# The rwkv scan of a two-block model: the two directions set eight steps apart, the backward preparation put behind the forward one, and the rates of the keys kept

## What is computed

```python
def _wkv7_step(S, inp):
    r, w, k, v, kk, a = inp
    sa = jnp.einsum('bhvk,bhk->bhv', S, kk)
    S = S * w[:, :, None, :] - sa[..., None] * (kk * a)[:, :, None, :] + v[..., None] * k[:, :, None, :]
    y = jnp.einsum('bhvk,bhk->bhv', S, r)
    return S, y
...
    decay = jnp.exp(-jnp.exp(w_log))
    a = jax.nn.sigmoid((a0[:, None, None, :] + la).astype(jnp.float32))
...
    kd = kf[None] * (1.0 + (a - 1.0) * k_a)
...
    _, y_fwd = lax.scan(_wkv7_step, S0, (r_t, tm(decay[0]), tm(kd[0]), v_t, kk_t, tm(a[0])))
    _, y_bwd = lax.scan(_wkv7_step, S0, (r_t, tm(decay[1]), tm(kd[1]), v_t, kk_t, tm(a[1])), reverse=True)
...
    kdh = (kd[0] + kd[1]).reshape(B, L, H, N)
    bonus = jnp.sum(rh * kdh * r_k, -1, keepdims=True) * v.reshape(B, L, H, N).astype(jnp.float32)
    out = ((y + bonus.reshape(B, L, D)) * g).astype(x.dtype)
```

## Time and profile before

| | |
|---|---|
| median of three runs | 2638.3 us (2636.0 to 2647.1) |
| the profiled execution | 2632.1 us, its span 2630.3 us |
| TensorE busy | 2522.9 us (96%), 23502 matmul records |
| VectorE, ScalarE, GpSimd busy | 1991.4, 1538.5, 52.5 us |
| mean granted clock of TensorE | 0.973 |
| chain that ended last | TensorE 88%, VectorE 6%, ScalarE 3%, DMA 1%, issue 1% |
| HBM | 533.8 MB read, 203 GB/s over the span |

### The profile page before, as it was taken

How to read it: one execution, slowest core, us unless ns; L and a number is a source line. 1 busy time by engine, 2 the same in 40 slices (tenths; PEclk the granted TensorE clock), 3 DMA queues, 4 the chain that set the end, 5 groups by cost and what they waited for, 6 DMA issues and landing times.

```text
span 2630.3 us, 54618 instructions
## 1 busy us (share of the span) xinstructions
PE 2522.9 (96%) x23502; PEld 2344.5 (89%) x23502; DVE 1991.4 (76%) x3044; ACT 1538.5 (58%) x2505; POOL 52.5 (2%) x58
## 2 busy tenths in 40 slices
PE   8999999988989999999999999999998899999999
PEld 8779998867887899999999999999897799998999
DVE  4545547765544699999999999999877788575884
ACT  4435435444423577777777777777665565464663
POOL 0001100000000000000000000000003000000000
PEclk9889999978998999999999999999999999999999
DMA  6123452300002499999999999999832255451443
GB/s 245 71 73 120 167 188 103 112 1 3 20 4 90 164 362 343 359 347 363 340 368 335 372 336 368 338 373 336 312 132 102 81 193 180 174 186 55 169 179 127
DMA packets 83258, 538.48 MB, mean 205 GB/s; under 512 B 9488, under 2 KB 9616, under 8 KB 38976
## 3 DMA queue, kind: packets, MB, share of 16 engines
q1 hardware_dynamic: 82368, 530.68, 54.7%
q0 software_dynamic: 640, 4.22, 0.4%
HBM read 533.81 MB, written 1.05 MB: 203 GB/s over the span
## 4 chain that ended last, share of the span: by engine, by line
PE 88%; DVE 6%; ACT 3%; issue 1%; DMA 1%; DVEq 0%; SPq 0%; PEldq 0%; ACTq 0%
PE ps L575 24%; PE ps L576 23%; PE ps L577 23%; PE ps L1465 2%; PE ps L581 1%; PE ps L590 1%; DVE sl L533 1%; PE ps L1995 1%; PE ps L1400 1%; PE ps L1450 1%; PE ps L1459 1%; PE ps L818 1%; PE ps L1421 1%; PE ps L2140 1%; PE ps L1443 1%
## 5 line engine op out<-in xcount | busy, mean ns | idle before, releaser
L2222 DVE TENSOR_TENSOR sl<-ring,sh 128x1024 fp32r<-128x1024 f32 x613 | 718.2, 1220 | 13.7 <-ACT sh L2180 10.9
L2180 ACT ACTIVATE sh<-ring 128x1024 fp32r<-128x1024 f32 x613 | 608.9, 1061 | 1.3 <-DVE xl L2065 1.3
L575 PE MATMUL ps<-sh,xh 128*128 128x256 f32 (+2 forms) x2012 | 568.9, 283 | 2.1 <-DVE sl L533 1.2
L577 PE MATMUL ps<-sh,xl 128*128 128x256 f32 (+2 forms) x2012 | 568.3, 282 | 0.0
L576 PE MATMUL ps<-sl,xh 128*128 128x256 f32 (+2 forms) x2012 | 567.9, 282 | 0.0
L575 PE MATMUL ps<-xh,sh 128*128 128x256 f32 (+2 forms) x1856 | 537.0, 289 | 24.5 <-DVE sl L533 12.8
L576 PE MATMUL ps<-xl,sh 128*128 128x256 f32 (+2 forms) x1856 | 532.0, 287 | 0.0
L577 PE MATMUL ps<-xh,sl 128*128 128x256 f32 (+2 forms) x1856 | 528.8, 285 | 0.0
L533 DVE TENSOR_TENSOR sl<-ring,sh 128x1024 fp32r<-128x1024 f32 (+1 forms) x341 | 401.0, 1201 | 80.9 <-ACT sh L526 80.5
L526 ACT ACTIVATE sh<-ring 128x1024 fp32r<-128x1024 f32 (+1 forms) x341 | 338.9, 1021 | 112.1 <-PE ps L577 105.4
L575 PEld LDWEIGHTS ps<-sh,xh 128*128 128x128 f32 x2012 | 378.3, 188 | 11.8 <-DVE sl L533 1.5
(11 more groups left out here) (552 smaller groups left out, 3887.2 us busy)
## 6 DMA issues: line engine op xcount, KB each, us to landing
ring<-ws_d SPq DMA_DIRECT2D x229, 1024.0 KB, 7.1
ring<-ws_d SPq DMA_DIRECT2D x80, 1536.0 KB, 6.4
ring<-ws_d SPq DMA_DIRECT2D x225, 512.0 KB, 6.5
ring<-ws_d SPq DMA_DIRECT2D x24, 1408.0 KB, 6.0
ring<-ws_d SPq DMA_DIRECT2D x4, 1256.0 KB, 5.6
ring<-ws_d SPq DMA_DIRECT2D x2, 1088.0 KB, 4.8
scan_t<-scn_d POOLq DMA_DIRECT2D x1, 1844.0 KB, 7.7
ring<-ws_d SPq DMA_DIRECT2D x1, 1248.0 KB, 5.2
```

What stands on the lines that cost most here:

```text
L575: e.matmul(out, ah, bh, start=start, stop=False)
L577: return e.matmul(out, al, bh, start=False, stop=stop)
L2180: e.activation(out, raw(u)[:, a:z], ACT.Copy).then_inc(*af.on("high", u, i))
L2222: e.tensor_tensor(l, raw(u)[:, a:z], f32(h), SUB).then_inc(s_fd if i < 2 else s_fp, 1)
```

## The change

The scan gets another order and the bonus another source for the rates.

- `streams`: six steps of forward alone, one of backward, four times backward and forward, one of backward; then the round with the bonus. At its beginning forward has done 10 steps and backward 6. Forward ends its short chunk in the first eight rounds, so that from then on it is eight steps behind backward, and the last eight rounds are forward's alone (75 rounds instead of 67).
- The rates are kept: forward's Sigmoid writes them to `Yb` (after the mix that still reads `DP` there), and backward's preparation adds its own (L1671 after the change). The bonus takes the sum from `Yb`, over 256 tokens instead of 272. Its two matmuls, two Sigmoids and the addition for each tile are gone, and it takes three rounds for a tile instead of four.
- The late mixes come in two lots of four instead of 3, 3 and 2.
- Unused matmuls: 12 behind forward's and 10 ahead of each direction's first G, where 20 stood ahead of forward's.

```diff
@@ -1151,7 +1151,7 @@
         def late_dve(w, e):
-            for ks in ((0, 1, 2), (3, 4, 5), (6, 7), (), (), ()):
+            for ks in ((0, 1, 2, 3), (4, 5, 6, 7), (), (), (), ()):
                 for k in ks:
@@ -1353,8 +1353,8 @@
-        PREPARE, LEAD = 6, 7
-        VV, va1, gate = KK, HW, Rr
+        PREPARE, LEAD = 6, 6
+        VV, gate = KK, Rr
         oc, nw = columns(out_weights())
@@ -1369,9 +1369,11 @@
                 next(runs[0])
-            for _ in range(PREPARE):
-                for g in (runs[0], runs[1], runs[0]):
-                    next(g)
+            next(runs[1])
+            for _ in range(PREPARE - 2):
+                next(runs[1])
+                next(runs[0])
+            next(runs[1])
             runs.append(bonus())
@@ -1401,9 +1403,10 @@
                 yield
+                if n == 0:
+                    warm_pe(w, e, "decays", 12)
                 yield
-                if n == 0:
-                    warm_pe(w, e, "prepared", 20)
+                warm_pe(w, e, ("prepared", n), 10)
                 w.wait_ge(dv["prepared", n, 1], IN_CON)
@@ -1514,18 +1517,10 @@
                 for k in range(8):
-                    for n in range(2):
-                        b, free = psum.take(("out a", n, k))
-                        w.wait_ge(*free)
-                        e.matmul(PS[:, b, 0:T0], sn("a2")[64 * n:64 * n + 64, 128 * k:128 * k + 128], HA[64 * n:64 * n + 64, :], start=True, stop=True).then_inc(
-                            *pe.on("out a", n, k))
                     yield
-                    if k:
-                        colsum_pe(w, e, ("quad", k - 1), "blk", VV[:, k - 1:k, :], 1, T0, dv["quad", k - 1])
-                    for _ in range(3):
-                        yield
-                yield
-                colsum_pe(w, e, ("quad", 7), "blk", VV[:, 7:8, :], 1, T0, dv["quad", 7])
+                    yield
+                    yield
+                    colsum_pe(w, e, ("quad", k), "blk", VV[:, k:k + 1, C0:T0], 1, T1, dv["quad", k])
                 for _ in range(BEFORE_GATES):
@@ -1547,10 +1542,12 @@
                     d0 = slice(4 * hf, 4 * hf + 4)
-                    t1, t2 = d.t1[hf], d.t2[hf]
+                    t1, t2 = d.t1[hf], d.t2[hf] if n else Yb[:, 4 * hf:4 * hf + 4, :]
                     for name, dst, bias in (("w2", t1, f"w0{n}"), ("a2", t2, f"a0{n}")):
...
                             w.wait_ge(pe[name, n, hf, i])
+                            if n == 0 and name == "a2":
+                                w.wait_ge(dv["mixed", 5, 4 * hf + i])
                             e.activation(dst[:, i, :], PS[:, psum[name, n, hf, i], 0:T0], ACT.Sigmoid, bias=par(bias)[:, 4 * hf + i:4 * hf + i + 1]).then_inc(
@@ -1622,17 +1619,10 @@
                 for k in range(8):
-                    for n, v in ((0, VV[:, k, :]), (1, va1)):
-                        w.wait_ge(pe["out a", n, k], dv["prepared", 1, 1], *([dv["out b", k - 1]] if n and k else []))
-                        e.activation(v, PS[:, psum["out a", n, k], 0:T0], ACT.Sigmoid, bias=par(f"a0{n}")[:, k:k + 1]).then_inc(*ac.on("out a", n, k))
-                        psum.gone["out a", n, k] = [ac.now()]
+                    w.wait_ge(dv["prepared", 1, 1])
+                    e.activation(VV[:, k, C0:T0], Yb[:, k, C0:T0], ACT.Identity, scale=par("k_a")[:, k:k + 1], bias=ka_rest2[:, k:k + 1]).then_inc(*ac.on("key of out", k))
                     yield
-                    yield
-                    w.wait_ge(dv["out b", k])
-                    e.activation(VV[:, k, :], VV[:, k, :], ACT.Identity, scale=par("k_a")[:, k:k + 1], bias=ka_rest2[:, k:k + 1]).then_inc(*ac.on("key of out", k))
-                    yield
-                    yield
-                for _ in range(BEFORE_GATES):
+                for _ in range(BEFORE_GATES + 16):
                     yield
@@ -1654,7 +1644,7 @@
                     d0 = slice(4 * hf, 4 * hf + 4)
-                    t1, t2 = d.t1[hf], d.t2[hf]
+                    t1, t2 = d.t1[hf], d.t2[hf] if n else Yb[:, d0, :]
                     A, B, K = d.AR[:, 0, d0, :], d.BK[:, 0, d0, :], d.BK[:, 1, d0, :]
@@ -1677,6 +1667,8 @@
+                    if n == 1:
+                        e.tensor_tensor(Yb[:, d0, C0:T0], Yb[:, d0, C0:T0], d.t2[hf][:, :, C0:T0], ADD).then_inc(*dv.on())
                     w.wait_ge(ac["decay", n, hf])
@@ -1757,24 +1749,20 @@
                     w.wait_ge(pe["quad", k])
-                    e.tensor_tensor(VV[:, k, :], PS[:, psum["quad", k], 0:T0], Vr[:, k, :], MUL).then_inc(*dv.on("bonus", k))
+                    e.tensor_tensor(VV[:, k, C0:T0], PS[:, psum["quad", k], 0:T1], Vr[:, k, C0:T0], MUL).then_inc(*dv.on("bonus", k))
                     psum.gone["quad", k] = [dv.now()]
...
                 for k in range(8):
-                    va = VV[:, k, :]
-                    yield
-                    w.wait_ge(ac["out a", 1, k])
-                    e.tensor_tensor(va, va, va1, ADD).then_inc(*dv.on("out b", k))
+                    va = VV[:, k, C0:T0]
                     quad(k - 1)
                     yield
+                    w.wait_ge(ac["key of out", k])
+                    e.tensor_tensor(va, va, Kr[:, k, C0:T0], MUL).then_inc(*dv.on())
+                    w.wait_ge(dv.now())
+                    e.scalar_tensor_tensor(out=va, in0=va, scalar=par("r_k")[:, k:k + 1], in1=Rr[:, k, C0:T0], op0=MUL, op1=MUL).then_inc(*dv.on("quad", k))
                     yield
-                    w.wait_ge(ac["key of out", k])
-                    e.tensor_tensor(va, va, Kr[:, k, :], MUL).then_inc(*dv.on())
-                    w.wait_ge(dv.now())
-                    e.scalar_tensor_tensor(out=va, in0=va, scalar=par("r_k")[:, k:k + 1], in1=Rr[:, k, :], op0=MUL, op1=MUL).then_inc(*dv.on("quad", k))
                     yield
-                yield
                 quad(7)
```

## The result

The changed kernel takes **2613.9 us** in the median (2611.8 to 2617.0), the kernel before 2637.2 in the runs beside it: a ratio of **0.991, interval 0.988 to 0.994**, 23 us less. The prediction was 2611, range 2598 to 2630, faster by over 0.5% with a chance of 0.86. The profiled execution of after took 2614.7 us (span 2612.9), that of before 2632.1 (span 2630.3).

What follows compares the result with a forecast made beforehand. Bound by an engine-to-engine chain up to 614 us, then by TensorE's throughput. 590.6 + 182.5 + 8 + 3 + 1 + 2 + 2 = 789.1 against 815.99, -26.9: 2605.2 traced, plus 6.2 gives 2611.4 us, range 2598 to 2630.

Steps and rivals of the forecast that it cites:

- The start of the loop: Up to the first backward G: the backward preparation's last VectorE product ends at 590.6 instead of 614.0, -23.4 us.
- the rival's 3 to 4 us: Backward preparation later, by lower clock or ScalarE's order: 596.5 instead of 590.6, total 2617; chance 0.12.
- TensorE's work: From the first backward G to the scan's end: 182.5 us, with 5.4 of recomputing matmuls gone and moved forward work added.
- Idle time: TensorE in the joint loop: 8 us of stalls, 3 of hops in forward's lone rounds, 1 at the end.
- The clock: Low TensorE clock in the loop: 2 us at the start, 2 for a later dip that costs 3.4 or 0.
- The offset and the stalls: Joint loop: eight steps' offset mixes small level matmuls with other groups; stalls 8 us, between 1 and 16.5.
- the sign: In the profile after, TensorE's "issue" idle in the loop would be down by half.
- Rival 1: Joint loop: stalls come with every instruction packet, not dense bursts; idle stays 16.5 us, total 2619; chance 0.16.
- Behind the scan: Output projection's weights, issued 1 us ahead of the scan's end, arrive in time: 0 us, a miss up to 2.
- Rival 4: Loop's G and Ut steps: VectorE's masks and copies delay the other direction; 34 us if uncovered, total 2645; chance 0.05.
- the 6.2 us that the sum adds for the median: Median of the runs shown lies 6.2 us above the profiled execution; added to 2605.2 it gives 2611.4.

Runs made afterwards that it cites:

- 18 fillers: The kernel after with 18 instead of 10 filler matmuls ahead of the first forward G: 2618.9 us, ratio 0.994 against the kernel before.
- the offset kernels: The kernel after and the variants with forward eight steps behind backward in the joint loop: ratios 0.989 to 0.994 against the kernel before.
- the two in step that lose least next to before: Kernel before with rates kept, bonus rhythm and gates' place as before; without fillers 2634.4 us, with two in each removed place 2637.0; both ratio 1.001.
- an offset loop: Kernel after with gate matmuls 15 rounds later, 18 fillers ahead of first forward G, eight more early in the joint loop: 2610.0 us, ratio 0.991.
- the order alone: Kernel before with the new order, mixes and fillers, but rates computed again for the bonus: 2617.1 us, ratio 0.993.
- the rates alone: Kernel before with rates kept and the bonus's shorter rhythm, in the old order, mixes and fillers: 2650.9 us, ratio 1.006.
- late gates and 18 fillers: Kernel after with gate matmuls 15 rounds later and 18 instead of 10 fillers ahead of the first forward G: 2605.7 us, ratio 0.989.
- the in-step kernel: Kernel after with nine more forward steps ahead of the joint loop, so the directions stand one step apart: 2647.4 us, ratio 1.004.

## Why the prediction came out right, and where it did not

- **The start of the loop** (-23.4 forecast) is right: 64.9 us against 63.6, the last VectorE product as the end of a sum of durations. The full clock there, which I expected, holds in one of four traces; where it doesn't, the rival's 3 to 4 us are due.
- **TensorE's work** (182.5): 194.3 us busy, less 10.6 lost to the clock, is 183.7. Right within 1.2.
- **Idle time** (8 of stalls, 3 of hops, 1 at the end): 19.0 measured. Stalls 9.5, for 8; ScalarE 6.6, of which 3.4 are gate copies that the sum did not have; VectorE 0.9 at the end and 1.0 within; the rest lies in gaps below a row's size. Too small by 7.
- **The clock** (2 + 2 us): 10.6 lost, too small by 6.6, and as a share the term that was mis-sized most. I priced two dips by their length in before and never asked what brings them. Why the late one is 15 us long stays open: the same rounds run at the full clock with 18 fillers.
- **The offset and the stalls: not borne out.** The sum took the offset to remove them. After has 9.5 us for before's 12.4, where half was named as the sign; but the offset kernels lie between 7.3 and 12.7, and the two in step that lose least next to before, at 10.7 and 10.8. The most, 12.7, belongs to an offset loop. A low clock does not explain the 7.3 of the order alone, which loses no more than 8.4 us to it. Rival 1's premise, a stall with every packet, is wrong (10 of after's 50, and 18 if waits from 0.15 us on are counted), but its idle time (16.5 us, of any kind) is nearer to the 19.0 than my 12: 14 to 19 us were idle in every version, in step or offset. The Trainium skill, "Runtime: NRT & Kernel Launch", Instruction fetch mechanics, which says that fetching is hidden, does not hold here: 12.4 us of before's loop, and 2.80 us in one piece with the rates alone.
- **Behind the scan** (0): right, 0.4 us less.
- **Rival 4** (coupling through VectorE) did not come: VectorE's share of TensorE's waits is 2.1 us, half of it at the loop's start.
- **Why the time was right all the same.** In part by luck. The traced execution was forecast at 2605.2 and took 2614.7, 9.5 us more: the loop 14.8 and the start 1.3 too long, of which 6 came back outside the scan and 0.4 behind it. Then the 6.2 us that the sum adds for the median did not come: after's median lies 0.8 below its traced execution. What is left is 2.5. So the two terms of the start (-22) and of the work (-6, and 8 moved in) stand, the terms for idling and the clock were 14 us too small together, and the right total does not bear them out.

## What to carry to other kernels

When a stream of small matmuls is near TensorE's limit, read the granted clock by stretches before pricing anything else, and ask of each edit in which rounds each group of matmuls and each wait then stands: at the same work that decided 12 to 16 us here, more than the 5.7 us of matmuls that the kept rates take away. Fillers in the places of the removed matmuls did not bring it back. An edit that "removes work" also moves what is counted in steps behind it, a weight load too. Measure the halves of a change each by itself before adding them. Work with slack, like the gate's matmuls, belongs where a chain runs alone (0.994 to 0.989 with 18 fillers).

## What the runs showed of the hardware

- The granted clock fell to 0.5 without one long pause. Ahead of the fall at 792 in before, TensorE was busy for 60 to 96% of each 2 us from 782 to 790, with gaps of 1.05, 0.54 and 0.80 us (all "issue") between small matmuls; the kernel after fell at 788, behind gaps of 0.81, 0.51 and 0.48. But such gaps do not always bring a fall (732 to 748 in before, and the whole loop behind 610 with late gates and 18 fillers); what decides was not found.
- It then stayed low through stretches in which TensorE was busy without a gap: 28.00 of 28 us at 0.52 (the in-step kernel, 632 to 660), 14.00 of 14 at 0.54.
- Waits for instructions end 1.2 to 1.6 us behind the landing of an instruction packet, in all 136 cases of 0.45 us or more; the longest are 1.4 us, and once 2.80 us, when the next packet started only at the end of a weight load of 1 MB. At the low clock there are hardly any.
- Where the falls stand differs between kernels whose loops are the same but start microseconds apart (the medians with 10 and with 18 fillers are 5 us apart, as much as the edits that were being told apart), and the scatter within a kernel goes with the clock: over the 23 executions of before beside the last group, time and mean granted clock have a correlation of -0.93 (2627.8 us at 0.972, 2648.7 at 0.960).
